# Block 2 up projections: one 512-column product for both parts of x, a bank for each channel tile

## The reference, cut to what matters

```python
h = rms_norm(x, norm_ffn_g[i])
a, b = jnp.split(h @ w_ffn_in[i], 2, axis=-1)      # w_ffn_in: 1024 x 5632
x = x + ((jax.nn.silu(a) * b) @ w_ffn_out[i]).astype(x.dtype)
```

## Time and profile before

| what | value |
|---|---|
| median of 3 runs | 2140.92 us |
| lowest, highest | 2139.42, 2144.38 us |
| the profiled execution, its own time | 2139.99 us |
| its span, from the first instruction to the last | 2137.9 us |
| around the span | 2.1 us |
| PE busy | 2042.9 us (96%) |
| POOL, ACT, DVE busy | 1624.0 (76%), 1070.5 (50%), 825.0 us (39%) |
| mean granted clock of TensorE | 0.986 |

### The profile page before, as it was taken

One profiled execution on the slowest core, in us unless ns is written; L12 is line 12 of the kernel. 1 busy time (PEld: TensorE's weight loads), 2 busy tenths in 40 slices (PEclk: granted clock), 3 DMA queues, 4 the chain that ended last, 5 costly groups with the idle time before them and its releaser, 6 DMA issues. The chain is left out here.

```text
span 2137.9 us, 33319 instructions
## 1 busy us (share of the span) xinstructions
PE 2042.9 (96%) x13064; PEld 1794.0 (84%) x13064; DVE 825.0 (39%) x1779; ACT 1070.5 (50%) x2073; POOL 1624.0 (76%) x1292
## 2 busy tenths in 40 slices
PE   8899999997889999999999989999999999899998
PEld 7688999896779899898778857998897788679996
DVE  4432465066541366254323173331341303643321
ACT  3344566453235466544454585544444554765443
POOL 6395898893368588999789617898897797268887
PEclk9899999997999999999999999999999999999999
DMA  8653555561035377555445614555554457235553
GB/s 292 119 178 119 171 184 178 185 198 66 1 118 178 100 245 220 185 177 188 138 148 191 219 41 138 178 183 181 174 192 158 134 185 227 73 108 180 186 178 108
DMA packets 244496, 343.19 MB, mean 161 GB/s; under 512 B 8787, under 2 KB 173747, under 8 KB 244213
## 3 DMA queue, kind: packets, MB, share of 16 engines
q1 hardware_dynamic: 232344, 331.35, 47.1%
q10 hardware_dynamic: 11997, 9.72, 2.4%
HBM read 336.85 MB, written 4.19 MB: 160 GB/s over the span
## 5 line engine op out<-in xcount | busy, mean ns | idle before, releaser
L1452 POOL TENSOR_TENSOR w_lo<-ring,w_hi 128x512 fp32r<-128x512 f32 (+1 forms) x1216 | 1578.8, 1314 | 422.0 <-ACT w_hi L1544 376.6
L1544 ACT ACTIVATE w_hi<-ring 128x512 fp32r<-128x512 f32 (+1 forms) x1216 | 759.0, 630 | 826.8 <-PE bank L755 341.1
L755 PE MATMUL bank<-x_hi,w_hi 128*128 128x256 f32 x2144 | 609.6, 284 | 3.7 <-POOL w_lo L1452 2.9
L758 PE MATMUL bank<-x_lo,w_hi 128*128 128x256 f32 x2144 | 607.2, 283 | 0.0
L759 PE MATMUL bank<-x_hi,w_lo 128*128 128x256 f32 x2144 | 607.1, 283 | 0.0
L755 PEld LDWEIGHTS bank<-x_hi,w_hi 128*128 128x128 f32 x2144 | 412.0, 192 | 7.1 <-POOL w_lo L1452 3.4
L758 PEld LDWEIGHTS bank<-x_lo,w_hi 128*128 128x128 f32 x2144 | 412.2, 192 | 0.3
L759 PEld LDWEIGHTS bank<-x_hi,w_lo 128*128 128x128 f32 x2144 | 412.0, 192 | 0.0
L782 PE MATMUL bank<-w_hi,x_hi 128*128 128x512 f32 (+1 forms) x752 | 302.8, 403 | 21.4 <-POOL w_lo L1452 15.7
L786 PE MATMUL bank<-w_hi,x_lo 128*128 128x512 f32 (+1 forms) x752 | 293.7, 391 | 0.0
L785 PE MATMUL bank<-w_lo,x_hi 128*128 128x512 f32 (+1 forms) x752 | 293.3, 390 | 0.0
(11 more groups left out here) (299 smaller groups left out, 2050.4 us busy)
## 6 DMA issues: line engine op xcount, KB each, us to landing
ring<-in_w_in SPq DMA_DIRECT2D x74, 1024.0 KB, 5.1
ring<-in_ffn_w_up SPq DMA_DIRECT2D x44, 1024.0 KB, 5.1
ring<-in_w_ffn_in SPq DMA_DIRECT2D x44, 1024.0 KB, 5.1
ring<-in_ffn_w_down SPq DMA_DIRECT2D x20, 1024.0 KB, 5.0
ring<-in_w_ffn_out SPq DMA_DIRECT2D x20, 1024.0 KB, 4.9
ring<-in_xattn_wkv SPq DMA_DIRECT2D x16, 1024.0 KB, 5.2
ring<-in_w_o_ret SPq DMA_DIRECT2D x16, 1024.0 KB, 4.8
ring<-in_od_w_in SPq DMA_DIRECT2D x12, 1024.0 KB, 5.2
```

The costliest lines, as they stand in the source:

```text
L755: m = mm(out_, view(w_hi)[:, k, :], x_hi[:, 4 * kh + k, :], start=start, stop=False)
L758: mm(out_, view(w_hi)[:, k, :], x_lo[:, 4 * kh + k, :], start=False, stop=False)
L1452: tt(view(w_lo), src, view(w_hi), ALU.subtract).then_inc(w_lo_ready, 1)
L1544: return A(o, i_, ACT.Copy, **kw)
```

## The change

For up units 1 to 10 of layers 2 and 3 (`WIDE`, 20 units), `x_hi` and `x_lo` become two halves of one tensor `x_pair`, at the place that they had. For each k-tile PE makes one product of `w_hi` with both parts of x, 512 columns that fill a whole bank: the left half sums `w_hi*x_hi`, the right half `w_hi*x_lo`. A second product of 256 columns adds `w_lo*x_hi` to the left half. A channel tile has a bank of its own, so a unit fills four banks: c = 0 and 2 as before, c = 1 and 3 in banks 4 to 7. DVE scales each half of each bank by `R_b`, the right one to `E`, and adds the two (`scale_wide`); the steps after it are done for each channel tile by itself, with 256 columns. Silu becomes two operations of 256 columns. The other units, the pieces, the roundings, the transfers and the order on ACT and POOL stay.

```diff
--- before.py
+++ after.py
@@ -212,8 +212,8 @@
         xnT = sb("xnT", [P, KT, SEQ])
 
 
-        x_hi = sb("x_hi", [P, KT, SEQ], F32R)
-        x_lo = sb("x_lo", [P, KT, SEQ], F32R)
+        x_pair = sb("x_pair", [P, 2, KT, SEQ], F32R)
+        x_hi, x_lo = x_pair[:, 0], x_pair[:, 1]
         w_hi = sb("w_hi", [P, HELD, PIECE], F32R)
         w_lo = sb("w_lo", [P, HELD, PIECE], F32R)
         xs = sb("xs", [P, TT, D])
@@ -538,6 +538,7 @@
         NARROW = {"2vv", "3vv"}
         BY_TOKENS |= NARROW
         SPLIT = BY_CHANNELS | BY_TOKENS | BY_ROWS
+        WIDE = {f"{L}up{j}" for L in (2, 3) for j in range(1, FF_UNITS)}
         AFTER_NORM = {"eq"} | {f"{L}up0" for L in range(4)} | {"2qr0", "3qr0"}
         FIRST_ROWS = {f"{L}down0" for L in range(4)} | {f"{L}oret0" for L in (2, 3)}
         LAST_ROWS = {f"{L}down{DOWN_UNITS - 1}" for L in range(4)}
@@ -760,6 +761,29 @@
                     if c % 2 and kh:
                         m.then_inc(full[b], 1)
 
+            def split_wide(name):
+
+                b0 = 2 * (index[name] % 2)
+                for p in range(PIECES):
+                    c, kh = channel_part(name, p)
+                    b = b0 + c // 2 + 4 * (c % 2)
+                    if kh == 0:
+                        B.take(pe, (name, c), b)
+                    split_piece(name, p)
+                    view = piece_of(name, 0, p)[1]
+                    both = bank[b][:, :].rearrange("p (a n) -> p a n", a=2)
+                    for k in range(4):
+                        kt, last = 4 * kh + k, kh == 1 and k == 3
+                        if last:
+                            mm(bank[b][:, 0:SEQ], view(w_lo)[:, k, :], x_hi[:, kt, :], start=False, stop=False)
+                        m = mm(both, view(w_hi)[:, k, :], x_pair[:, :, kt, :], start=kt == 0, stop=last)
+                        if k == 0:
+                            m.then_inc(piece_started, 1)
+                        if not last:
+                            mm(bank[b][:, 0:SEQ], view(w_lo)[:, k, :], x_hi[:, kt, :], start=False, stop=False)
+                    if kh:
+                        m.then_inc(full[b], 1)
+
             def split_token_major(name, x_hi, x_lo, key=None, second_half=None, after=None, made=None):
                 b0 = 2 * (index[name] % 2)
                 n = VALUES if name in NARROW else PIECE
@@ -821,6 +845,8 @@
             def channel_major(name, xT, tiles=4, width=512, finish=True, **kw):
 
 
+                if name in WIDE:
+                    return split_wide(name)
                 if name in SPLIT:
                     return split_channel_major(name, *xT, **kw)
                 s, b0 = unit_at(name)
@@ -1944,10 +1970,15 @@
                     if j >= 2:
                         act.wait_ge(ff_h, L * FF_UNITS + j - 1)
                     act.wait_ge(ff_scaled, 2 * (L * FF_UNITS + j) + 1)
-                    evacuate((f"{L}up{j}", 0), g_s[j % 2][:, 0:2, :], func=ACT.Silu)
+                    if f"{L}up{j}" in WIDE:
+                        for c in range(2):
+                            b = B.uses[(f"{L}up{j}", c)][0]
+                            A(g_s[j % 2][:, c, :], bank[b][:, 0:SEQ], ACT.Silu).then_inc(empty[b], 1)
+                    else:
+                        evacuate((f"{L}up{j}", 0), g_s[j % 2][:, 0:2, :], func=ACT.Silu)
                 for j in range(DOWN_UNITS):
                     round_weights(f"{L}down{j}")
-            B.wait_full(act, (f"3up{FF_UNITS - 1}", 1))
+            B.wait_full(act, (f"3up{FF_UNITS - 1}", 3))
             act.dma_start(gain_row, I["norm_final_g_2"].rearrange("(o n) -> o n", o=1).broadcast_to([P, D])).then_inc(gain_loads, 16)
 
 
@@ -2215,6 +2246,19 @@
                 v = bank[b][:, :].rearrange("p (a b) -> p a b", a=2)
                 tt(v, v, two(R_b[:, :]), ALU.mult).then_inc(ff_scaled, 1)
 
+            def scale_wide(name, cs):
+
+                for c in cs:
+                    b = B.uses[(name, c)][0]
+                    B.wait_full(dve, (name, c))
+                    tt(E[:, c, 0:SEQ], bank[b][:, SEQ:2 * SEQ], R_b[:, :], ALU.mult)
+                    tt(bank[b][:, 0:SEQ], bank[b][:, 0:SEQ], R_b[:, :], ALU.mult)
+                drain()
+                for c in cs:
+                    b = B.uses[(name, c)][0]
+                    m = tt(bank[b][:, 0:SEQ], bank[b][:, 0:SEQ], E[:, c, 0:SEQ], ALU.add)
+                m.then_inc(ff_scaled, 1)
+
             def split_hidden(v, hi, lo, j):
 
                 drain()
@@ -2619,6 +2663,25 @@
                 norm(f"{L}f")
                 spread_rstd(f"{L}f")
                 for j in range(FF_UNITS):
+                    if f"{L}up{j}" in WIDE:
+                        scale_wide(f"{L}up{j}", (0, 1))
+                        scale_wide(f"{L}up{j}", (2, 3))
+                        for c in range(2):
+                            B.wait_emptied(dve, (f"{L}up{j}", c))
+                        drain()
+                        products = [bank[B.uses[(f"{L}up{j}", 2 + c)][0]] for c in range(2)]
+                        for c in range(2):
+                            tt(products[c][:, 0:SEQ], products[c][:, 0:SEQ], g_s[j % 2][:, c, :], ALU.mult)
+                        drain()
+                        for c in range(2):
+                            nc.vector.tensor_copy(g_hi[:, 2 * j + c, :], products[c][:, 0:SEQ])
+                        drain()
+                        for c in range(2):
+                            tt(g_lo[:, 2 * j + c, :], products[c][:, 0:SEQ], g_hi[:, 2 * j + c, :],
+                               ALU.subtract).then_inc(empty[B.uses[(f"{L}up{j}", 2 + c)][0]], 1)
+                        drain()
+                        nc.vector.tensor_copy(small[:, 22, 0:1], small[:, 23, 0:1]).then_inc(ff_h, 1)
+                        continue
                     for q in range(2):
                         scale_bank((f"{L}up{j}", q))
                     B.wait_emptied(dve, (f"{L}up{j}", 0))
```

## The result

The changed kernel is slower: a ratio of 1.0024 to the kernel before, 95% interval 1.0015 to 1.0034, which on 2143 us is 5.1 us (3.2 to 7.3). The medians of 14 runs each are 2149.17 and 2143.22 us. The prediction was 2137.0 us, range 2133.0 to 2144.5, with no change inside 0.2% as the likeliest outcome; the time lies outside the range and on the other side of before. The forecast was set off from 2140.92 us, the median of 3 runs of before; that of the 14 is 2.3 us higher, and this part of the distance has nothing to do with the change.

What follows compares the result with a forecast made beforehand. PE was taken to bound the kernel, busy 96% of the span. Each layer would save 4.05 us and lose 2.1, so 3.9 us off 2140.92 in two layers: 2137.0 us, range 2133 to 2144.5.

Steps and rivals of the forecast that it cites:

- Part 1: PE in the up units: one 512-column product at 0.2267 us replaces two of 0.120, saving 0.0133 us a k-tile.
- the chain: Steps on DVE and ACT from Silu of unit 9 to Silu of unit 10, ahead of the down projection; 3.84 us before.
- the rival at 0.2333: The 512-column product takes 0.2333 us, as in the down units: 2.0 saved against 2.1 lost, 2141 us; chance 0.15.
- The rule that I kept as a rival: Product spacing is columns over clock plus 2.5 ns, so merging saves 2.5 ns a k-tile: 2143.6 us; within a 0.13 case.
- Part 2: DVE's steps in a wide unit grow from 3.7 to 7.5 us, hidden under PE's 11.1 inside units 1 to 9.
- Part 3: DVE's longer steps before the down projection add 2.1 us in each layer, bounds 1.6 to 2.5.
- The stall: PE's idle between up unit 10 and the down projection, forecast to grow from 1.6 to 3.9 us.
- The clock: Rival: PE's clock falls behind the longer stall, losing about 1.5 us a layer: 2138.5 or 2140 us; chance 0.20.
- The forecast case: The 512-column product takes 0.2267 to 0.229 us and the clock is kept; chance 0.42, own range 2135 to 2139 us.

Runs made afterwards that it cites:

- e4: The changed kernel with 15 products of 512 columns of zeros on PE between the last up unit and the down projection; 0.9997 of the kernel before.
- e8: The changed kernel run and profiled once more, with no further edit; 1.0023 of the kernel before.
- e1: The changed kernel, but ACT rounds the first three pieces of `down0` before Silu of unit 10, not after; 0.9950 of the kernel before.
- e10: The changed kernel with three pieces of `down0` rounded before Silu of unit 10 and each piece's wide products grouped; 0.9963 of the kernel before.
- e6: The changed kernel with `x_pair` laid out so both parts of a k-tile lie side by side; 1.0009 of the kernel before.

## Why the prediction was wrong

- **Part 1, the price of a 512-column product: this term was mis-sized, and it is the step that failed first.** I took 0.2267 us, from the row with the same tensors in exchanged roles, and had 0.2333 and 0.240 beside it. It is 0.235, and the 256-column product beside it 0.118, not 0.120. The saving up to the chain was to be 4.05 us a layer; the 80 pieces gained 2.4, without the length of the last product, so the 76 up to the chain some 2.3. With the clock kept (e4) the stage gains 0.4 us in all and not 3.9, so this term alone takes away nearly the whole forecast gain. PE is nearest to the rival at 0.2333, to which I gave 0.15. I had written that the kernel is slower from 0.2336 us a product on; by the 2.1 us of the chain, spread over 304 k-tiles, it is 0.2331. The rule that I kept as a rival (a saving of 2.5 ns a k-tile, by the Trainium skill, TensorE: Matmul & The Clock Gate, section Back-to-back issue gap, which calls it the gap of a product by itself) is not what the trace has either: 360 to 352.5 ns, a saving of 7.5.
- **Part 2, DVE's load and POOL: right in kind, DVE's price somewhat high.** A pair of narrow operations with its drain costs 0.83 to 0.85 us, a unit 6.6 us on DVE where 7.5 was forecast (54.09 us in a window of 8.2 units), and POOL's remainder stayed at 1293 ns. The scalings that write back to the bank, which I had at 0.42, take 0.33 from start to start (1467.14 - 1466.81). Nothing inside units 1 to 9 waited for either engine.
- **Part 3, the chain: right in place and size.** 1.90 us longer where 2.1 was forecast. The stall that I put at 3.9 us began at the end of the last up product: counted so it is 3.98 - 0.235 = 3.74 us.
- **The clock: the step that turned no gain into a loss.** I had the fall of the clock as a rival for 0.20 and its price at 1.5 us a layer. The price was about right, measured at 1.4 to 2.7 us. The chance was far off: of the 12 idles of 3.65 to 4.02 us in the six profiles that had them unfilled, the clock fell behind 11. Behind those of 1.7 and 2.0 us it never did. The forecast case needed the clock to stay, and the rows that I had, 1.7 us without a fall and nearly 6 with one, gave no ground to call staying twice as likely. I also counted the rivals one at a time. Both came together, the dearer product and the fall of the clock in both layers; from my own prices that is 2141 + 3 = 2144 us, and no case had it. (The chance of over 0.2% faster was added up wrong too: half of 0.42, a fifth of 0.20 and 0.07 are 0.32 and not 0.34.)
- **The sum again, with measured terms:** 2.5 saved, 2.3 and 1.5 lost, a loss of 1.2 to 1.3 us a layer in the first profile; for both layers 2.4 us in the first profile and 3.6 in the second. The timed 5.1 us (3.2 to 7.3) is a little more. The rest goes, as far as the record shows, with half clock outside the stage, which my sum had no term for. By the mean granted clocks of all executions of e8 (0.9795) and of before beside it (0.9829), TensorE was at half clock for 14.7 us more. 10.2 us of that lie in e8's two stages, 4.5 outside; at 0.36 us each (estimate, from the twelve profiles ahead of layer 2's `R_b`) these are 1.6 us, and 3.6 + 1.6 = 5.2 where 4.9 was timed. The same working gives -11.0 for e1 (timed -10.7) and -7.5 for e10 (timed -7.9), so it is also a part of why these two missed their expected ratios; in all ten runs e1 to e10 it comes within 0.7 us of the timed difference. It was made after the runs, and one profile stands for each kernel's stage. Whether the change itself brings more half clock elsewhere isn't shown.
- **What I didn't ask:** the chain begins with DVE's steps on unit 9, so making them longer was costly only because ACT's queue had the next stage's rounding behind Silu of unit 10. I named that queue and didn't price the order as a choice. With it changed the same wide product is a gain.

## What to carry to other kernels

Work that is hidden in the middle of a stage is not hidden at its end: look for the last unit, follow the queue of each engine from there into the next stage, and put what the next stage needs first ahead of what waits. An idle of PE of some 4 us cost more than itself here, by 1.4 to 2.7 us in 11 of 12 cases, so in a sum add what the clock takes behind it, and treat it as likely once the idle is clearly longer than those behind which the trace shows the clock kept. A duration from a product with the operands' roles exchanged is a bound at best, not a price: 0.227 in one set of roles, 0.235 in the other.

## What was not expected of the hardware

- Products of 512 columns with x moving and the weights stationary took 0.224 to 0.241 us from start to start, in a pattern that repeats, with a median of 0.235; the same tensors in exchanged roles took 0.227. Neither one stretch nor two in the moving operand made a difference, and their order in a piece made a part of it.
- The 256-column products beside them came to 0.113 to 0.121 us, where in the kernel before they were 0.120 (two of 1916 at 0.119).
- After an idle of 4 us PE worked at half clock in one down projection and at full clock in the other of the same execution (e6).
- Where two profiles differ by several us in a stretch whose code is the same, the time at half clock differs with them: layer 2's `R_b` at 1350.8 us with 51.2 us of half clock ahead of it, at 1357.5 with 71.7.
